# Five small changes of order in a two-layer hybrid encoder step (latent attention, RG-LRU, squared-ReLU MLP)

## The reference

```python
z = rmsnorm(x, norm_mix_g) @ w_in          # 1024 -> 768 | 256 | 32 | 512 | 512
q = rmsnorm(c_q) @ w_uq ; ckv = rmsnorm(c_kv) ; kpe = rope(k_r)
y = rg_lru(conv4(x_r)) * gelu(g_r)         # two 512x512 block-diagonal gates, a scan over tokens
o = softmax(chunk_causal(q_nope @ k_nope + q_pe @ kpe)) @ v      # 8 heads
h = x + concat(rmsnorm(o), rmsnorm(y)) @ w_out
x = h + square(relu(rmsnorm(h) @ w_up)) @ w_down                 # 1024 -> 4096 -> 1024
```

## Time and profile before

| what | value |
|---|---|
| median of 3 runs | 2488.35 us (2484.24 to 2490.82) |
| the profiled execution, its own time | 2484.64 us |
| its span, first to last instruction | 2482.8 us |
| granted TensorE clock, mean | 0.998 |
| TensorE busy | 2460.0 us (99%) |
| VectorE, ScalarE, GpSimd busy | 1784.7, 1222.0, 541.1 us |
| HBM traffic | 94 GB/s over the span |

### The profile page before, as it was taken

How to read it: one execution, slowest core, us unless ns; L and a number is a source line. 1 busy time by engine, 2 the same in 40 slices (tenths; PEclk the granted TensorE clock), 3 DMA queues, 4 the chain that set the end, 5 groups by cost and what they waited for, 6 DMA issues and landing times.

```text
span 2482.8 us, 43928 instructions
## 1 busy us (share of the span) xinstructions
PE 2460.0 (99%) x17424; PEld 2371.4 (96%) x17424; DVE 1784.7 (72%) x2750; ACT 1222.0 (49%) x2197; POOL 541.1 (22%) x506
## 2 busy tenths in 40 slices
PE   9999999999999999999999999999999999999998
PEld 9999977899999999999999998779999999999997
DVE  8678766578866676677676797664887766776676
ACT  5455355435554455455524644554355554544455
POOL 0024155101112211221201232441012112211222
PEclk9999999999999999999999999999999999999999
DMA  4122201213447645764822222013236457646755
GB/s 160 54 60 72 61 11 38 89 57 109 98 93 148 127 95 101 145 119 95 232 81 60 61 66 59 11 38 97 60 110 120 99 115 134 118 98 117 134 116 173
DMA packets 108570, 237.73 MB, mean 96 GB/s; under 512 B 15265, under 2 KB 18433, under 8 KB 108369
## 3 DMA queue, kind: packets, MB, share of 16 engines
q0 software_dynamic: 47680, 96.48, 22.9%
q1 hardware_dynamic: 60544, 138.42, 17.7%
q10 hardware_dynamic: 144, 0.04, 0.0%
HBM read 151.37 MB, written 81.18 MB: 94 GB/s over the span
## 4 chain that ended last, share of the span: by engine, by line
PE 86%; DVE 5%; DMA 5%; issue 3%; ACT 1%; POOL 1%; SPq 0%; DVEq 0%; ACTq 0%; POOLq 0%
PE ps L959 27%; PE ps L1304 20%; PE ps L1353 18%; PE ps L1168 5%; PE ps L1183 4%; DMA raw_all<-in_wst 4%; PE ps L1445 2%; PE ps L1238 2%; PE ps L1115 2%; PE ps L1416 1%; DVE wlo L2809 1%; PE ps L1026 1%; PE ps L1140 1%; PE ps L1047 1%; DVE raw_all L2933 1%
## 5 line engine op out<-in xcount | busy, mean ns | idle before, releaser
L1974 ACT ACTIVATE whi<-raw_all 128x512 fp32r<-128x512 f32 (+1 forms) x420 | 249.3, 600 | 351.1 <-DVE raw_all L2933 129.3
L2809 DVE TENSOR_TENSOR wlo<-raw_all,whi 128x512 fp32r<-128x512 f32 (+1 forms) x420 | 271.5, 652 | 197.2 <-ACT whi L1974 193.2
L3303 POOL DMA_DIRECT2D x_scratch<-stage x224 | 198.6, 930 | 685.6 <-DVE stage L2943 538.0
L2027 ACT ACTIVATE stage<-ps 128x536 f32<-128x536 f32 (+1 forms) x224 | 135.3, 610 | 109.8 <-PE ps L1353 104.5
L1497 ACT ACTIVATE whi<-raw_all 128x1024 fp32r<-128x1024 f32 (+3 forms) x72 | 66.6, 926 | 234.0 <-PE ps L959 231.4
L2943 DVE TENSOR_TENSOR stage<-stage,ps 128x536 f32<-128x536 f32 (+1 forms) x168 | 118.9, 708 | 86.2 <-PE ps L1353 85.2
L2519 DVE TENSOR_REDUCE mxp<-ps 64x1 f32<-64x64 f32 (+11 forms) x384 | 140.4, 372 | 54.7 <-PE ps L1115 48.2
L959 PE MATMUL ps<-xgh,whi 128*128 128x358 f32 (+1 forms) x720 | 157.3, 327 | 0.0
L959 PE MATMUL ps<-xgl,whi 128*128 128x358 f32 (+1 forms) x720 | 156.6, 325 | 0.0
L959 PE MATMUL ps<-xgh,wlo 128*128 128x358 f32 (+1 forms) x720 | 156.5, 325 | 0.0
L3288 POOL DMA_DIRECT2D raw_all<-in_wst x58 | 62.6, 1079 | 392.2 <-DMA raw_all<-in_wst 267.9
(11 more groups left out here) (834 smaller groups left out, 7661.0 us busy)
## 6 DMA issues: line engine op xcount, KB each, us to landing
raw_all<-in_wst SPq DMA_DIRECT2D x232, 256.0 KB, 3.5
raw_all<-in_wst SPq DMA_DIRECT2D x80, 512.0 KB, 3.6
x_scratch<-stage POOLq DMA_DIRECT2D x112, 268.0 KB, 5.9
x_scratch<-stage POOLq DMA_DIRECT2D x112, 264.0 KB, 5.8
raw_all<-in_wst POOLq DMA_DIRECT2D x58, 256.0 KB, 5.2
x_scratch<-xall POOLq DMA_DIRECT2D x24, 537.0 KB, 3.5
xall<-x_scratch SPq DMA_DIRECT2D x24, 537.0 KB, 9.0
xall<-in_xT SPq DMA_DIRECT2D x16, 537.0 KB, 7.2
```

Of the source, the lines that this page charges most:

```text
L1974: nc.scalar.activation(dst, src, ACT.Copy).then_inc(S["u_hi"], 1)
L2027: nc.scalar.activation(quarters(stage_of(L, g, i, n)[:, 0:N2]), src, ACT.Copy, scale=-1.0 if row else 1.0).then_inc(S["x_copy"], 1)
L2809: V.tensor_tensor(dst, src, hi.bitcast(F32), ALU.subtract).then_inc(S["u_lo"], 1)
L3303: pool.dma_start(x_scr[2 * i + row, :, a:b], stage_of(L, g, i, n)[:, 0:b - a], accum_op=ALU.add).then_inc(S[done], 16)
```

## The change

It alters orders only; no instruction is added or removed. (1) In a group `copy(0, 1)` moves ahead of `copy(0, 2)` and of fill 5. (2) In a group `part_out(0, "P4")` moves ahead of fill 20. (3) In the second layer `mix_sum` moves from before product XR[1] to behind the first 9 of its 72 matmuls. (4) `max_step(0, 7)` to `(0, 10)` each move one value tile ahead, so that steps 6 and 7 both stand behind tile 0; `max_rows(0)` moves from behind tile 5 to behind tile 4. (5) `add_y(2)` moves ahead of `divide(3)`.

```diff
 ORDER = {
-    "p_copy": [(0, 0), (0, 2), (0, 1), (1, 0), (1, 1), (1, 2)],
+    "p_copy": [(0, 0), (0, 1), (0, 2), (1, 0), (1, 1), (1, 2)],
...
                     product(to_slot(U_XR[0]), U_XR[0], B_XR[0], 0, XH, XL, x_ready)
-                    mix_sum()
-                    product(to_slot(U_XR[1]), U_XR[1], B_XR[1], 0, XH, XL)
+                    product(to_slot(U_XR[1]), U_XR[1], B_XR[1], 0, XH, XL, lambda k: mix_sum() if k == 1 else None)
...
                     mm.then_inc(S["mm"], 1)
-                    if t + 6 < NMX:
-                        max_step(0, t + 6)
-                    if t == 5:
+                    if t == 0:
+                        max_step(0, 6)
+                    if t + 7 < NMX:
+                        max_step(0, t + 7)
+                    if t == 4:
                         max_rows(0)
...
                     copy(0, 0)
+                    copy(0, 1)
                     copy(0, 2)
                     fill(5)
-                    copy(0, 1)
...
                     part_out(1, "P1")
+                    part_out(0, "P4")
                     fill(20)
-                    part_out(0, "P4")
...
                 split(31)
+                add_y(2)
                 divide(3)
-                add_y(2)
                 o_low(3)
```

## The result

The changed kernel takes 2491.32 us (median of 9 runs, 2489.25 to 2495.93), the kernel before 2484.15 us on the same chip (9 runs, 2482.25 to 2490.82). The ratio is 1.0028, with a 95% interval of 1.0020 to 1.0037: 7 us slower. The forecast was 1.9 us faster. Its time of 2486.4 us had a range up to 2491.0, and the measured median lies 0.3 us beyond that. The miss is larger than those 0.3 us say: the forecast started from 2488.35 us, the median of three runs of the kernel before, and nine runs put that kernel at 2484.15 us. As a change of the kernel before, the forecast was 1.9 us faster and the measurement is 7 us slower.

A forecast was written before the change was run, and what follows sets the result against it. TensorE was taken as the bound, busy 2460.0 of 2482.8 us, leaving 22.8 us to win. Edits 1 to 5 summed -3.3 - 1.0 + 1.1 + 1.3 + 0 = -1.9 us, from 2488.35 to 2486.4 us; range 2481.0 to 2491.0.

The forecast's parts named there:

- both idle times: TensorE's idle time before product b22, which reads b4h: 1.3 us in the first layer, 2.0 in the second.
- Does the earlier pair of additions bring the reload sooner?: Edit 2: whether two additions to x, issued 1 us sooner, speed SyncE's reload of weight quarters before P6; taken as -1.0 us.
- ends of -4.1 and +0.8: Edit 2's bounds: reload 1 us sooner in each group, -4.1 us; or 0.1 us later wherever P6 waits, +0.8.
- the share of 0.82 in a half microsecond: DMA engines only 0.82 busy, moving 88 GB/s, just before the additions are under way; read as slack they would fill.
- the fourth rival: Edit 2: additions issued ahead of pair 3's reload hold it back; 1 us later gives +11.7, 2500.0 us; chance 0.03.
- the first rival: Edit 2: reload indifferent to the additions, lands 0.1 us later by fill 21's delay; costs 0.8, 2488.2 us; chance 0.28.
- the next thing that is late: Edit 3: XR[1] waits for next_split(1)'s low weights until 1254.2, 1.1 us longer than for the last next_sum; +1.1 us.
- the end of +2.5: Edit 4's upper bound over both layers: +2.5 us, with another 0.5 us before the scores in each.
- an end of -1.3 a layer: Edit 5's bound: -1.3 us a layer if add_y(3), for which OY[5] waits, does come sooner.

The follow-up runs named there:

- With the additions 1 us behind it: Edit 2 alone, with GpSimd's first addition held until VectorE has made fill 21 (additions issued at 3.33 us); 2481.13 us, ratio 0.9983 against the kernel before.
- The timed parts: Two runs against the kernel before: edit 2 alone, 2491.37 us, ratio 1.0024; edits 1, 3, 4 and 5 without edit 2, 2484.92 us, ratio 0.9991.
- the hold at 2.2 us: Edit 2 alone, with GpSimd's additions held until ScalarE's fill 21 (issued at 2.24 us); 2482.13 us, ratio 0.9991 against the kernel before.
- the five of the table: Additions' issue behind the copy of P1: edit 2 alone 1.4 us; holds 1.9, 2.2, 3.3; kernel before 2.4. Ratios 1.0024, 0.9999, 0.9991, 0.9983, 1.
- one wait of GpSimd: All five edits, with GpSimd's additions held until VectorE has made fill 21; 2480.55 us, ratio 0.9983 against the kernel before; the changed kernel stood at 1.0028.
- edits 3 and 5 with their covers moved along: Kernel before with edits 3 and 5, next_split(1) and add_y(3) earlier, sum behind 18 matmuls, table load behind shift_hi(0); 2482.20 us, ratio 0.9992.

## Why the prediction was wrong, step by step

**Edit 1: right.** Forecast -3.3 with both idle times gone; measured -3.7 (interval -6.0 to -1.5), and none is left. In group 1 after, `copy(0, 1)` starts at 700.16 us and `copy(0, 2)` at 703.13 us, with 1.78 and 2.35 us of waiting before them where one wait of 4.75 us was the earlier trace rows:

```profile
700.16 0.62 ACT L1999 ACTIVATE f0t4hf<-ps 128x536 f32<-128x536 f32 x1 [1.78 <-PE ps L1305]
703.13 0.62 ACT L1999 ACTIVATE f0t3lf<-ps 128x536 f32<-128x536 f32 x1 [2.35 <-PE ps L1305]
```

**Edit 2: this is the step that failed**, the answer to "Does the earlier pair of additions bring the reload sooner?" The prediction took -1.0 us with ends of -4.1 and +0.8. Measured: +6.0 us alone, and +7.0 us of idle time in the trace after. (P6 waits in 9 of the 14 groups before, where the prediction counted 7 or 8, which changes little.) All that leads up to the question was right: the copy and the additions came 1 us sooner, and `block_sum(3, 0)` was the place to look at. The answer had the wrong sign. It reasoned that the additions would fill unused time (the share of 0.82 in a half microsecond) and be out of the way sooner. That half microsecond was a poor sample, and its slack was taken. In the kernel before, from 831.06 us to the reload's issue at 833.20 us, the software queue, with two earlier additions issued at 827.36 and 828.95 us, alone fills the engines' time:

```profile
q0 software_dynamic: 191, 0.38, 101.0%
q1 hardware_dynamic: 33, 0.05, 8.2%
```

Then these run out, and the packets of the new additions have not begun. The half microsecond of the earlier trace rows lies in this gap, 3.0 to 3.5 us behind the copy, and it is the reload that uses it. Packets begun in each us (software queue, hardware queue; mean of the 14 groups, from the packet records of the traces):

| us behind the copy of P1 | 2 to 3 | 3 to 4 | 4 to 5 | 5 to 6 |
|---|---|---|---|---|
| before | 84, 0 | 11, 67 | 25, 88 | 46, 38 |
| after | 94, 1 | 45, 0 | 65, 12 | 40, 99 |

With the additions 1 us sooner the gap is closed, and the reload's packets begin more than 1 us later. And the additions in question are in flight for 6.3 to 6.6 us, longer than the reload, so 1 us sooner does not get them out of its way; it puts them in front. A half microsecond with 0.18 unused is no room for 2 x 268 KB.

The row that should have been weighed is the landing time of the reload beside that of the additions, in the kernel before: 4.6 us for 256 KB, beside a median of 3.5 us for all such loads on the page:

```profile
raw_all<-in_wst SPq DMA_DIRECT2D x232, 256.0 KB, 3.5
```

With the additions 1 us behind it the same transfer takes 3.0 us, so the reload was already late by 1.6 us in that group.

The mechanism is the fourth rival, "the additions, issued ahead of the reload of pair 3, hold it back", which had a chance of 0.03. Its price for each us of lateness holds. In the trace after, by groups 0 to 6 of the first layer, us behind the copy of P1:

| group | 0 | 1 | 2 | 3 | 4 | 5 | 6 |
|---|---|---|---|---|---|---|---|
| `block_sum(3, 0)` starts | 8.56 | 10.45 | 9.48 | 9.42 | 9.68 | 9.55 | 9.30 |
| idle before P6 | 0 | 1.82 | 0.85 | 0.33 | 1.04 | 0.93 | 0.67 |

Up to 8.6 us nothing is lost, then nearly each us costs one. The rival supposed the reload 1 us later in every group, priced that at 12.6 us and came to 2500.0. `block_sum(3, 0)` starts 0.6 us later on the mean of the 14 groups, and the idle time before P6 grows by 7.0 us. So the rival had the direction right and the size nearly twice too large, and the forecast had the sign wrong.

Of the first rival (the reload is indifferent) nothing is left. The Trainium skill ("DMA: Bandwidth & Descriptors", section "Queues, rings and completion order"), which stands behind it, says that an engine alternates packet by packet between the queues with work. Here, in the 2.4 us from the reload's issue on, the packets of its queue and of the software queue go from 125 against 93 to 3 against 160. From 3 to 4 us behind the copy, on the mean of 14 groups, the reload's queue then begins next to no packet (0.3) while the software queue begins 45. The reload's turns do depend on whether the additions came first, and the measurement decides against the use made of that rule. Whether what the page calls a packet is what the profile counts as one is not shown. Whether the additions' packets occupy the engines, or what they read and write in HBM does, no run here separates.

**Edit 3: right.** Forecast +1.1, with the low weights as the next thing that is late. After, VectorE makes them, and XR[1] waits until then; `mix_sum` has no wait of its own:

```profile
1256.94 1.22 DVE L3087 TENSOR_TENSOR wlo<-raw_all,whi 128x1024 fp32r<-128x1024 f32 x1
...
1258.21 0.76 PE L959 MATMUL ps<-xgh,whi 128*128 128x358 f32 x3 [1.75 <-DVE wlo L3087]
1259.79 2.04 PE L976 MATMUL ps<-msq,ones 128*128 128x512 f32 x6
```

The weight loads show 2.04 us in place of 0.91 before the same point: +1.1. With the low weights made sooner, the wait is gone altogether.

**Edit 4: right in kind, too small by 1.0 us.** Forecast +0.6 to 0.7 in each layer. In the first, step 7 waits 0.70 us for the reduction, and head 0's scores 0.55 in place of 0.18 us, of which 0.22 comes back before head 1. In the second, the scores wait 1.38 us in place of 0.99, and the steps 1.0 us. That makes some 0.9 and 1.4 us, +2.3 in place of +1.3, inside the end of +2.5.

```profile
293.68 0.19 PEld L1114 LDWEIGHTS ps<-keh,qe 96*128 96x128 f32 x1 [0.70 <-DVE mxp L2520]
...
1545.96 0.30 PEld L1184 LDWEIGHTS ps<-qe,keh 97*128 97x128 f32 x2 [1.38 <-issue]
```

**Edit 5: right in the first layer, missed in the second.** Forecast 0, with an end of -1.3 a layer. In the first layer OY[4] has no wait, and OY[5] one of 1.48 us in place of 1.02 + 0.29, since `add_y(3)` stands behind `o_low(3)` as before:

```profile
486.13 1.27 DVE L2554 TENSOR_TENSOR o<-o,rc 128x1072 f32<-128x1072 f32 x1 [2.86 <-issue]
490.08 2.85 DVE L2225 SCALAR_TENSOR_TENSOR ol<-o,vecs,oh 128x1074 fp32r<-128x1074 f32 x1 [2.67 <-ACT osqt L1785]
493.45 1.26 DVE L2609 TENSOR_TENSOR xall<-xall,ps 128x1074 f32<-128x1074 f32 x1
...
494.83 0.46 PEld L959 LDWEIGHTS ps<-yh,whi 128*128 128x128 f32 x3 [1.48 <-issue]
```

In the second layer neither has one: the OY weight loads had 1.1 us of idle time (1700 to 1745 us in the kernel before) and have none after (1705 to 1750 us). The prediction read the first layer only; why the two layers differ was not followed up. Together the edit gives 0.9 us.

```profile
L959 PEld LDWEIGHTS ps<-yh,whi 128*128 128x128 f32 x87 | 14.7, 189 | 1.1 <-issue 1.1
...
L959 PEld LDWEIGHTS ps<-yh,whi 128*128 128x128 f32 x90 | 15.3, 189 | 0.0
```

**The sum again.** With what the traces show, -3.3 + 7.0 + 1.1 + 2.3 - 0.9 = +6.2 us, beside the -1.9 of the forecast and the +7.0 of the timed runs. Edit 2 makes 8.0 us of the difference of 8.1; the misses of edits 4 and 5, +1.0 and -0.9, cancel by luck.

**What stays open.** The timed parts, +6.0 and -2.2 us, add up to +3.8, where the whole change measures +7.0 with an interval from +5.0 to +9.2; the parts' own intervals, some 2 us wide to each side, allow for that, and no further interaction is shown. The last group of the second layer keeps a late reload in most kernels (2.81 us before); what is different there was not tried, nor why the kernel before does no better than the hold at 2.2 us. Other issue times than the five of the table were not tried either, so 3.3 us is not shown to be the best.

## What to carry to other kernels

Work that becomes ready sooner on one engine also releases its DMAs sooner, and these can land in front of a load that somebody waits for: when a step is moved, list the transfers that it lets go, and compare their issue with that of the next load on the critical path. If they can wait, try them behind it, until a copy waits for the tile that they free; here one wait of GpSimd was worth 11 us, where the five edits together had cost 7. And when a step is moved away from a wait, ask what it covered, and move that too: edits 3, 4 and 5 cost 2.5 us together, and edits 3 and 5 with their covers moved along, and a moved table load in place of edit 4, stood 4.5 us below that.

## What was not expected of the hardware

Two accumulating DMAs of 268 KB on the software queue that are issued 1 us ahead of two plain loads of 256 KB on the hardware queue slow the loads from 3.0 us (additions 1 us behind) to 5.7 us (ahead) in group 2, while they themselves take 5.5 and 6.6 us. For both the time in flight is shorter in the later order. In the 2.4 us behind the loads' issue their queue gets 125 packets through with the additions beside them, and 3 with the additions ahead. The software queue's bytes are also dearer, by the recorded time of their packets: in the three stretches of 4.4 us it takes 129 to 159% of the 16 engines' time for each MB (in the stretch after, 101.7% for 0.64 MB), the hardware queue 79 to 91% (5.5% for 0.07 MB).
